# Shifting the sample window caches: the same sixteen copies, issued in the retention heads instead of the delta heads

## The reference, cut to what matters

```
kcat = jnp.concatenate([kbuf, dk], 1)
vcat = jnp.concatenate([vbuf, dv], 1)
...
kbuf_new, vbuf_new = kcat[:, -wb:], vcat[:, -wb:]
```

## Time and profile before

| | |
|---|---|
| median of 3 runs | 4620.56 us (4617.07 to 4631.93) |
| the profiled execution | 4621.08 us, its span 4619.3 us |
| PE busy | 4132.8 us, 89% of the span |
| DVE, ACT, POOL busy | 38%, 21%, 3% |
| mean granted TensorE clock | 0.941 |
| the sixteen copies | 4088 KB each, issued by ACT between 137.4 and 969.4 us |
| where the blocks begin | `heads_A` at 137 us, `heads_B` at 1262 us |

### The profile page before, as it was taken

The page is one execution under the profiler, slowest core; times in us unless marked ns, Lnnn a source line. Parts: engine busy times, 40 slices in busy tenths (PEclk is TensorE's granted clock), DMA queues, the critical chain, the costliest instruction groups (busy, mean ns, idle before and its releaser), DMA issues. The chain is left out here.

```text
span 4619.3 us, 59156 instructions
## 1 busy us (share of the span) xinstructions
PE 4132.8 (89%) x23986; PEld 2533.9 (55%) x23986; DVE 1742.9 (38%) x3961; ACT 960.9 (21%) x1526; POOL 146.7 (3%) x67
## 2 busy tenths in 40 slices
PE   4897988979799899799999999999999997889897
PEld 2474674746655555454565656666565655444443
DVE  2363563735512321312242433425151525444442
ACT  3221332313301101111122222222222223000111
POOL 0000000000000000000000000000000000000000
PEclk8898989989899899899999999999999998999896
DMA  4406033050200210310011010101010102789886
GB/s 104 155 6 187 5 66 122 6 187 6 39 12 28 33 25 21 99 45 1 14 52 37 19 37 19 37 19 37 19 45 11 56 12 81 251 292 311 289 287 215
DMA packets 250756, 379.32 MB, mean 82 GB/s; under 512 B 23369, under 2 KB 154766, under 8 KB 247786
## 3 DMA queue, kind: packets, MB, share of 16 engines
q1 hardware_dynamic: 190358, 185.86, 14.5%
q10 hardware_dynamic: 51408, 157.31, 10.0%
q0 software_dynamic: 8720, 32.38, 2.0%
HBM read 327.90 MB, written 114.56 MB: 96 GB/s over the span
## 5 line engine op out<-in xcount | busy, mean ns | idle before, releaser
L475 PE MATMUL ps<-xT,big 128*128 128x416 f32 x2560 | 919.0, 521 | 78.3 <-DVE raw L490 62.0
L1554 PE MATMUL ps<-xT,big 128*128 128x416 f32 x2560 | 902.2, 513 | 0.0
L475 PEld LDWEIGHTS ps<-xT,big 128*128 128x128 f32 x2560 | 495.1, 194 | 499.3 <-issue 428.1
L1554 PEld LDWEIGHTS ps<-xT,big 128*128 128x128 f32 x2560 | 484.5, 190 | 396.3 <-issue 396.2
L1680 DVE TENSOR_TENSOR big<-ps,rstd 128x416 f32<-128x416 f32 x160 | 94.6, 591 | 801.2 <-PE ps L1554 801.2
L1603 PE MATMUL ps<-vtok,wt 128*128 128x128 f32 x2176 | 297.6, 280 | 30.9 <-DVE wt L1746 30.1
L2055 PE MATMUL ps<-o_words,big 128*128 128x512 f32 x512 | 286.7, 649 | 28.4 <-DMA o_words<-scr_o 14.4
L1578 PE MATMUL ps<-big 128*128 128x512 f32 (+3 forms) x640 | 290.3, 536 | 6.5 <-DVE vtok L1690 6.5
L1603 PEld LDWEIGHTS ps<-vtok,wt 128*128 128x128 f32 x2176 | 265.4, 192 | 53.3 <-DVE wt L1746 51.0
L1375 PE MATMUL ps<-big,wout 128*128 128x416 f32 x640 | 227.3, 518 | 18.3 <-DMA big<-scr_o 18.3
L2146 DVE STREAM_TRANSPOSE big<-rstd 128x512 f32<-128x512 f32 x312 | 206.9, 690 | 63.1 <-DMA rstd<-in_cache_fox_k 47.2
(11 more groups left out here) (403 smaller groups left out, 4699.8 us busy)
## 6 DMA issues: line engine op xcount, KB each, us to landing
rstd<-in_cache_fox_k SPq DMA_DIRECT2D x256, 256.0 KB, 4.2
vring<-in_cache_fox_v ACTq DMA_DIRECT2D x256, 256.0 KB, 4.6
out_win_k_sample<-in_cache_win_k ACTq DMA_DIRECT2D x8, 4088.0 KB, 28.9
out_win_v_sample<-in_cache_win_v ACTq DMA_DIRECT2D x8, 4088.0 KB, 41.2
big<-in_w_in_even SPq DMA_DIRECT2D x32, 512.0 KB, 11.1
big<-in_w_in_odd SPq DMA_DIRECT2D x32, 512.0 KB, 6.7
o_words<-scr_o POOLq DMA_DIRECT2D x8, 2048.0 KB, 11.7
rstd<-in_cache_win_k SPq DMA_DIRECT2D x56, 256.0 KB, 6.4
```

The costliest lines, as they stand in the source:

```text
L475: last = pe.matmul(k.ps[banks[at % 2]][:, 0:CH], k.w[:, j, m * P:(m + 1) * P], k.xT[:, j, n * CH:(n + 1) * CH], start=(j == 0), stop=(j == ...
L1554: last = pe.matmul(k.ps[PBANK[at % 2]][:, 0:CH], k.w[:, j, m * P:(m + 1) * P], k.xT[:, j, n * CH:(n + 1) * CH], start=(j == 0), stop=(j == ...
```

## The change

The four issues are taken out of the loop over the delta heads (`h` in `heads_A`) and put at the top of the loop over the retention heads (`u` in `heads_B`), with the same sequences, cuts and semaphore.

```diff
@@ heads_A, scalar
             for h in range(H):
 
-                for b in (h, h + H):
-                    for dst, src in ((io.out_win_k_sample, io.cache_win_k), (io.out_win_v_sample, io.cache_win_v)):
-                        act.dma_start(dst[0, bass.ds(b, 1), 0:WBUF - L].rearrange("b (g r) h d -> (b g) (r h d)", g=28),
-                                      src[0, bass.ds(b, 1), L:WBUF].rearrange("b (g r) h d -> (b g) (r h d)", g=28)).then_inc(k.windows_shifted, 16)
                 for m in range(2):
@@ heads_B, scalar
             for u in range(H):
+                for b in (u, u + H):
+                    for dst, src in ((io.out_win_k_sample, io.cache_win_k), (io.out_win_v_sample, io.cache_win_v)):
+                        act.dma_start(dst[0, bass.ds(b, 1), 0:WBUF - L].rearrange("b (g r) h d -> (b g) (r h d)", g=28),
+                                      src[0, bass.ds(b, 1), L:WBUF].rearrange("b (g r) h d -> (b g) (r h d)", g=28)).then_inc(k.windows_shifted, 16)
                 silu_gate(act, k, s["proj_taken"], s["gate_b"], PROJ * u)
```

## The result

The changed kernel takes 4537.86 us (median of 4 runs, 4536.1 to 4544.33), against 4620.07 before: ratio 0.982, 95% interval 0.980 to 0.984. That is 82 us faster where 70 were forecast, at the lower edge of the range. Run again later beside other runs of the kernel before, it took 4540.43 against 4619.41: 0.9834 (0.982 to 0.9849), or 79 us. Its first profiled execution took 4539.22 us, span 4537.4. Two of the six runs of one kernel further down (copies in mid-head 4) were slow, at 6158.87 and 15597.28 us, and its median in the table is that of the other four.

What follows compares the result with a forecast made beforehand. PE, busy 89% of the span, bounds the kernel, standing still at three delta-head seams for stores held by copies. Removing 25.2 + 19.7 + 25.2 = 70.1 us from 4621.1 gives 4551.0 us, range 4537 to 4568.

Steps and rivals of the forecast that it cites:

- the sum: Whole program: the profiled execution, 4621.1 us, less 70.1 us at the seams between delta heads is 4551.0 us.
- The copies hold the store: Seams between delta heads: the old head's second store takes about 28 us beside the copies, under 3.7 us alone.
- The three seams: Where one delta head follows another: PE's third projection piece ends 25.2, 19.7 and 25.2 us earlier, sum 70.1 us.
- The store lands in under 3.7 us and DVE is ready before PE: First seam between delta heads: without copies the first bank is empty by 408.1, before PE needs it at 410.08.
- Nothing to gain in the first head, nothing to pay in the retention heads: First delta head gains 0; copies added to the retention heads cost 0, with 44 us of cover for late stores.
- late `ret`: First retention head: the `ret` load falls behind the copies and DVE stops for 14.7 us; 4565.7 us, chance 0.08.
- another cause of the wait: Seams between delta heads: something else, for instance `g_row`, holds the stores; time stays at 4621 us, chance 0.04.
- the wait one block later: Three retention-head seams: late stores stop DVE before the clearing of `R`, 28 us each; 4635 us, chance 0.03.

Runs made afterwards that it cites:

- copies in mid-head 4: The changed kernel with the copies of index 3 issued in the fourth delta head instead, about 95 us into it; 4537.87 us, ratio 0.9817.

## Why the prediction was right or wrong

The direction, the place and the mechanism at the seams were right, and the time is at the lower edge of the range; the sum missed 12 us of 82. Point by point:

- *The copies hold the store* was right: no copies, a wait for the stores, and a later issue each bring DVE's wait to 3 us.
- *The three seams*, 25.2 + 19.7 + 25.2 = 70.1, measured 26.6 + 21.0 + 25.5 = 73.0 in the first profile and 71.2 with the second. The error of 1 to 3 us lies in PE's first two pieces, which the forecast kept at 12.87, 14.30 and 11.69 us; DVE took the second 11.5, 13.1 and 11.4 us after PE's start (11.4, 13.4 and 13.0 in the second profile). The rows below the list show why for the first seam.
- *The store lands in under 3.7 us and DVE is ready before PE* was right in what counts: 3.0 us in the first profile and up to 4.5 in the second, and PE set the pace at all three seams of both.
- *Nothing to gain in the first head, nothing to pay in the retention heads* was right. `ret` landed in 3.9 us, `R0` was issued at 1415.3 (forecast 1493, less the 76 us by which everything had moved up, is 1417), and nobody waited. The rivals with a late `ret`, with another cause of the wait, and with the wait one block later all fall.
- *The step that failed is the sum*, 4621.1 - 70.1: it took the rest of the program to move up as it stood, and put what lies outside the seams at nothing. Of the measured 79 to 82 us some 8 to 9 are not at the seams. About 4 are the end of the fourth delta head, where POOL's scaling and DVE's products meet within a microsecond: the trace of the kernel before had the 8.10 us of L937 at that place, but the forecast read no row there and did not ask what stretched them. The rest, 5.7 us in the first pair of profiles, is in the output projection and the last stretch, which differ as much between two executions of one kernel; what of it repeats is not shown. That the range reaches down to the measured time is luck: its lower end comes from the 83.7 us that DVE waited, a bound on the seams, and the seams gave 73.0.

PE's first 3 us on the projection at the first seam, before and after, with the columns of the earlier trace rows:

```profile
397.21:400.21 3.00, 3.00 (x6) 1.58 (x5) 0.00 (x0) 2.73 (x3) 0.00 (x0) 0.50 1.63 552
...
399.80:402.80 3.00, 3.00 (x10) 1.72 (x9) 0.00 (x0) 2.72 (x3) 0.00 (x0) 0.95 0.66 248
```

The granted clock was 0.50 (the level of 1.2 GHz) there before and 0.95, almost all at 2.4 GHz, after: six matmuls against ten. In the 10 us ahead of it, with the same work on PE, it was 0.50 in both. At the third seam of the second profile it was 0.50 in these 3 us, so this part of the seams differs between executions of one kernel.

## What to carry to other kernels

A bulk copy that nobody waits for is not free at a place where a small store must land before an engine may go on: look at which transfers are in flight on the other queues there, and issue the copy behind the store or in a stretch where nothing waits for a DMA. How long the small transfer waits is set by the size of the copy's pieces and by the number of its own and of those ahead of it in its queue, not by the bytes of either; cutting the copy into smaller pieces brought most of what moving it did, 64 of 73 us at the seams, at the price of issue time. When a stall is removed, ask of the stretches behind it which of them hang on two engines meeting within a microsecond, and give the range room for them.

## What the runs showed of the hardware that was not expected

- Where it was looked at, two queues took turns piece by piece, whatever the sizes of the pieces: 128 rows of 3328 bytes went beside 128 packets of copies in 64 KB pieces (19 us), and 254 pieces of 512 bytes beside 269 such packets (44 us). So a store of 128 rows (416 KB) waits 28 us beside these copies; beside the same bytes in 2 KB pieces it waits 7.
- While POOL scales the weights, operations that DVE begins with both inputs in SBUF stand still, and those that read PSUM do not: a product of 32x512 that takes 0.67 us took 7.5 beside it (8.10 for the two of L937), one of 128x1024 took 7.06 instead of 1.21, and one of 128x512 with an input in PSUM took 0.68 beside it as without it. Those that stood still ended 0.5 us (32x512) and 1.1 us (128x1024) after POOL.
- A delay of some 5 us in one engine's last products made the kernel before 35 us slower (4656 against 4621), because three stores of a head were then issued behind the copies instead of one.
